# Expert stage of a mixture-of-experts decoder step: lists two steps ahead, rows fetched in mid-step, down projection by rows in split halves

## The reference

```python
gprob = softmax(x @ w_rg + b_rg); gp, gidx = top_k(gprob, 1)            # 1 of 4 groups
ep, eidx = top_k(softmax(expert logits of that group), 2)               # 2 of its 4 experts
weights = gp * ep / sum(ep)
# for each of 16 experts, c = its column of the combine weights (0 where it wasn't chosen)
y = (silu(x @ w_gate) * (x @ w_up)) @ w_down                            # 1024 -> 512 -> 1024
acc = acc + c[:, None] * y
out = rmsnorm(x_residual + acc, final_g)
```

## Time and profile before

| | us |
|---|---|
| median of 3 runs | 1002.19 |
| lowest and highest | 999.67, 1006.11 |
| the profiled execution's own time | 999.66 |
| its span, first to last instruction | 997.9 |
| first gate product of the expert stage | 499.78 |
| TensorE busy, share of the span | 910.3, 91% |
| VectorE | 465.1, 47% |
| ScalarE | 307.9, 31% |
| GpSimd | 202.3, 20% |

### The profile page before, as it was taken

One profiled execution on the slowest core, in us unless ns is written; L12 is line 12 of the kernel. 1 busy time (PEld: TensorE's weight loads), 2 busy tenths in 40 slices (PEclk: granted clock), 3 DMA queues, 4 the chain that ended last, 5 costly groups with the idle time before them and its releaser, 6 DMA issues. The chain is left out here.

```text
span 997.9 us, 15701 instructions
## 1 busy us (share of the span) xinstructions
PE 910.3 (91%) x5829; PEld 788.3 (79%) x5829; DVE 465.1 (47%) x1168; ACT 307.9 (31%) x625; POOL 202.3 (20%) x255
## 2 busy tenths in 40 slices
PE   5998999999999699997199999999999999999992
PEld 3577775666667487885199999999999999999992
DVE  4428634436864444644634434444434444433342
ACT  5546214333535422543002221222221222221121
POOL 1000000000000100000123334443334443334441
PEclk9998999999998799998599999999999999999997
DMA  8410005101010280733147698777798777798750
GB/s 269 130 43 21 22 1 126 43 1 43 1 43 1 74 310 1 279 144 106 54 162 252 239 310 280 255 241 272 266 320 275 262 255 270 254 321 298 252 175 29
DMA packets 126885, 167.05 MB, mean 167 GB/s; under 512 B 14996, under 2 KB 98040, under 8 KB 126853
## 3 DMA queue, kind: packets, MB, share of 16 engines
q1 hardware_dynamic: 111493, 136.03, 41.0%
q0 software_dynamic: 15360, 30.59, 9.0%
HBM read 147.39 MB, written 41.17 MB: 189 GB/s over the span
## 5 line engine op out<-in xcount | busy, mean ns | idle before, releaser
L1649 PE MATMUL bank<-xT,ring 128*128 128x160 f32 x2048 | 287.4, 301 | 0.7 <-issue 0.7
L1649 PEld LDWEIGHTS bank<-xT,ring 128*128 128x128 f32 x2048 | 280.8, 191 | 3.4 <-issue 3.1
L419 PE MATMUL bank<-hT,ring 128*128 128x384 f32 (+1 forms) x480 | 152.5, 472 | 0.0
L1658 PE MATMUL bank<-hid,wdn 128*128 128x160 f32 x1024 | 147.0, 299 | 0.0
L1658 PEld LDWEIGHTS bank<-hid,wdn 128*128 128x128 f32 x1024 | 140.9, 190 | 0.0
L419 PEld LDWEIGHTS bank<-hT,ring 128*128 128x128 f32 x480 | 90.6, 192 | 53.6 <-issue 4.1
L1568 POOL DMA_INDIRECT out<-ot,lists_out x64 | 87.8, 1371 | 19.8 <-issue 19.8
L1754 ACT ACTIVATE sg<-bank 128x160 f32<-128x160 f32 x64 | 19.4, 303 | 212.1 <-PE bank L1649 207.8
L1851 DVE TENSOR_TENSOR hid<-sg,bank 128x160 f32<-128x160 f32 x64 | 20.6, 321 | 111.4 <-ACT sg L1754 111.3
L1869 DVE COPY yT<-bank 128x256 f32<-128x256 f32 x32 | 13.6, 424 | 121.5 <-PE bank L1658 121.5
L1236 PE MATMUL bank<-whi,ahi 128*128 128x512 f32 (+1 forms) x144 | 57.7, 401 | 6.7 <-DVE wlo L1347 6.6
(11 more groups left out here) (316 smaller groups left out, 1311.8 us busy)
## 6 DMA issues: line engine op xcount, KB each, us to landing
wdn<-in_w_down SPq DMA_DIRECT2D x32, 1024.0 KB, 8.2
ring<-in_w_gate SPq DMA_DIRECT2D x32, 1024.0 KB, 6.3
ring<-in_w_up SPq DMA_DIRECT2D x32, 1024.0 KB, 12.3
x<-in_x_prompt SPq DMA_DIRECT2D x16, 512.0 KB, 7.0
ring<-in_w_in SPq DMA_DIRECT2D x8, 1024.0 KB, 8.8
ring<-in_w_out SPq DMA_DIRECT2D x4, 1024.0 KB, 4.9
h_rows<-h SPq DMA_DIRECT2D x8, 512.0 KB, 2.6
sums<-x SPq DMA_DIRECT2D x8, 512.0 KB, 3.6
```

The lines of the kernel that those rows point to most:

```text
L419: mm = nc.tensor.matmul(acc(n)[:, 0:tn], ring[:, u % 4, k, c0:c0 + P], hT[:, k, t0:t0 + tn], start=k == 0, stop=k == KC - 1)
L1649: x = nc.tensor.matmul(bank[f % 2][:, side * 256:side * 256 + W], ring[:, u, k, c0:c0 + P], xT[:, k, :], start=k == 0, stop=k == KC - 1)
L1658: x = nc.tensor.matmul(bank[2 + j % 2][:, q * 256:q * 256 + W], wdn[:, d // 4, k * 512 + (d % 4) * P:k * 512 + (d % 4 + 1) * P], hid[:, k, ...
```

## The change

The expert stage is moved by one step, and the down projection is turned round.

- Lists are made two steps ahead. `lists` and `weight` now belong to the expert after the next; copies `lists_next` and `lists_now` follow. VectorE computes `indices(i + 2)` at the end of step i, after waits for `old` and for the rows of `xg`, and before `z2`. The one-hot comparison stands behind the second `hid`.
- GpSimd fetches `old` straight after the scatters, once z has landed in `sums`, without waiting for the scatters of `ot`. It fetches `xg` last, for the expert two steps ahead.
- The down projection of the main rows gives rows: the stationary operand is `hid` (128 rows), the moving one `wdn`, 512 columns. Both are split into a rounded half and the rest (`wdhi`, `wdlo`, `hs`, type fp32r), and three products of the halves replace one float32 product: 2 x 4 x 3 = 24 products. ScalarE makes the rounded halves, VectorE the differences.
- The leftover rows' down projection is four strips of 32 columns of the array (`left_down`), in float32, 16 products of 256 columns.
- The transposes back, `yT` and `yT2` are gone. `left_sums` moves from the next step's first gate product to the end of its own step.
- Down weights are loaded as two halves of the hidden rows, so that one DMA run is 4 KB instead of 2 KB, both after the leftover product and the last difference.
- `old`, `z`, `ot`, `squares` and `gfb` lie in memory that held the residual rows.

```diff
@@ expert_unit
-    return wdn[:, u - 4, :].rearrange("p (k n) -> p k n", k=4), w[e, :, :, (u - 4) * 512:(u - 3) * 512]
+    return wdn[:, u - 4, :].rearrange("p (k n) -> p k n", k=2), w[e, :, 2 * (u - 4):2 * (u - 3), :]
@@ sync
-                sp.wait_ge(e_gu if u < 4 else e_yt, i * 4 + (2 if u in (0, 1, 4) else 4))
+                if u < 4:
+                    sp.wait_ge(e_gu, i * 4 + (2 if u < 2 else 4))
+                elif u == 4:
+                    sp.wait_ge(e_yl, i + 1)
+                    sp.wait_ge(e_wl, i * 4 + 4)
@@ gpsimd, the loop
             hold()
-            send(1, sums_dram, N, z, z2, e_out)
+            send(1, sums_dram, N, z, z2[:], e_sum)
             send_results(e_out)
             pool.wait_ge(e_hold, i * 3 + 4)
-            pool.wait_ge(e_idx, i + 3)
-            pool.wait_ge(e_xt, i * 3 + 6)
+            pool.wait_ge(e_next, i * 2 + 4)
+            pool.wait_ge(e_sum, i * 32 + 32)
+            hold()
+            rows_old()
+            pool.wait_ge(e_out, i * 64 + 64)
+            pool.sem_inc(e_free, 1)
+            pool.wait_ge(e_hold, i * 3 + 5)
+            pool.wait_ge(e_idx, i + 4)
+            pool.wait_ge(e_xt, i * 3 + 9)
             hold()
             rows_x()
-            pool.wait_ge(e_out, i * 96 + 96)
-            pool.sem_inc(e_free, 1)
-            pool.wait_ge(e_hold, i * 3 + 5)
-            pool.wait_ge(e_now, i * 2 + 4)
-            hold()
-            rows_old()
@@ tensor
+        def down(h, k):
+            hi, lo = hs[:, k, 0, :], hs[:, k, 1, :]
+            whi, wlo = [w[:, k, h * 512:(h + 1) * 512] for w in (wdhi, wdlo)]
+            nc.tensor.matmul(bank[2 + h][:, :], hi, whi, start=k == 0, stop=False)
+            nc.tensor.matmul(bank[2 + h][:, :], hi, wlo, start=False, stop=False)
+            x = nc.tensor.matmul(bank[2 + h][:, :], lo, whi, start=False, stop=k == 3)
+            if k == 3:
+                x.then_inc(e_y, 1)
+        def left_down():
             for k in range(4):
+                for j in range(4):
+                    at = (k % 2) * D + j * CW
+                    x = nc.tensor.matmul(bank[1][W2 * j:W2 * (j + 1), 0:CW], hid[:, k, P:W],
+                                         wdn[:, k // 2, at:at + CW], start=k == 0, stop=k == 3)
+            x.then_inc(e_yl, 1)
@@ tensor, step: after the four gate and up products
+            pe.wait_ge(e_oh, i + 3)
+            pe.wait_ge(e_idx, i + 2)
+            indices()
+            pe.wait_ge(e_xg, i * 16 + 32)
+            rows_in(i * 16 + 32)
+            pe.wait_ge(e_h, i * 4 + 5)
+            left_down()
+            for h in range(2):
+                for k in range(4):
+                    if h == 0:
+                        pe.wait_ge(e_wl, i * 4 + k + 1)
+                        pe.wait_ge(e_hl, i * 4 + k + 1)
+                    down(h, k)
+            pe.wait_ge(e_xe, i * 3 + 6)
+            pe.wait_ge(e_sql, i + 1)
+            left_sums()
@@ scalar, in the loop over f, after Silu
+                for k in ((0,), (1,), (2, 3), ())[f]:
+                    if k % 2 == 0:
+                        act.wait_ge(e_w[4 + k // 2], i * 16 + 16)
+                    nc.scalar.copy(wdhi[:, k, :], wdn[:, k // 2, (k % 2) * D:(k % 2 + 1) * D]).then_inc(e_wh, 1)
+                act.wait_ge(e_h, i * 4 + f + 2)
+                nc.scalar.copy(hs[:, f, 0, :], hid[:, f, 0:P]).then_inc(e_hh, 1)
@@ vector
+        def gated_lo(i, f):
+            dve.wait_ge(e_hh, i * 4 + f + 1)
+            nc.vector.tensor_tensor(hs[:, f, 1, :], hid[:, f, 0:P], hs[:, f, 0, :].bitcast(F32),
+                                    ALU.subtract).then_inc(e_hl, 1)
+        def weights_lo(i, k):
+            dve.wait_ge(e_wh, i * 4 + k + 1)
+            nc.vector.tensor_tensor(wdlo[:, k, :], wdn[:, k // 2, (k % 2) * D:(k % 2 + 1) * D],
+                                    wdhi[:, k, :].bitcast(F32), ALU.subtract).then_inc(e_wl, 1)
@@ vector, in the loop over f, after hid
+                gated_lo(i, f)
+                for k in ((0,), (1,), (2, 3), ())[f]:
+                    weights_lo(i, k)
+                if f == 1:
+                    dve.wait_ge(e_rk, i + 2)
                     dve.wait_ge(e_ix, i + 2)
-                    indices(i + 1)
                     onehot((i + 2) % NE)
@@ vector, after x_out
             dve.wait_ge(e_free, i + 1)
+            dve.wait_ge(e_next, i * 2 + 2)
+            nc.vector.tensor_copy(lists_now[:], lists_next[:]).then_inc(e_now, 1)
+            nc.vector.tensor_copy(weight_now[:], weight_next[:]).then_inc(e_now, 1)
+            dve.wait_ge(e_now, i * 2 + 2)
             dve.wait_ge(e_old, i * 32 + 32)
+            dve.wait_ge(e_xg, i * 16 + 32)
+            dve.wait_ge(e_xl, i * 16 + 32)
+            dve.wait_ge(e_idx, i + 2)
+            nc.vector.tensor_copy(lists_next[:], lists[:]).then_inc(e_next, 1)
+            nc.vector.tensor_copy(weight_next[:], weight[:]).then_inc(e_next, 1)
+            dve.wait_ge(e_next, i * 2 + 4)
+            dve.wait_ge(e_ix, i + 3)
+            indices(i + 2)
```

More of the change, by code:

```diff
@@ L113, in program @@
                sums_dram, rank_m, table, iota_w, steps, once)
-        b3_all(nc, A, O, sb, sem, e_w, ring, wdn, bank, ident, eps_c, h2_dram, sums_dram, rank_m, table, iota_w, steps, once)
+        b3_all(nc, A, O, sb, sem, e_w, ring, wdn, bank, ident, eps_c, x1, h2_dram, sums_dram, rank_m, table, iota_w, steps, once)
 def b1_all(nc, A, O, S0, Sp, s_w, halves, sb, sem, bank, ident, onesf, eps_c, uT, gT, ring, x1, w_in, w_out, x_rows, cols):
@@ L1465, in expert_unit, with b3_all @@
     w = A["w_down"].rearrange("l e (k p) n -> (l e) p k n", p=P)
-    return wdn[:, u - 4, :].rearrange("p (k n) -> p k n", k=4), w[e, :, :, (u - 4) * 512:(u - 3) * 512]
-def b3_all(nc, A, O, sb, sem, e_w, ring, wdn, bank, ident, eps_c, h2_dram, sums_dram, rank_m, table, iota_w, steps, once):
+    return wdn[:, u - 4, :].rearrange("p (k n) -> p k n", k=2), w[e, :, 2 * (u - 4):2 * (u - 3), :]
+def b3_all(nc, A, O, sb, sem, e_w, ring, wdn, bank, ident, eps_c, rows, h2_dram, sums_dram, rank_m, table, iota_w, steps, once):
     c3 = ExitStack()
@@ L1492, in b3_all @@
     hid = sb("hid", [P, 4, W], ctx=c3)
-    yT = sb("yT", [P, KC, P], ctx=c3)
-    yT2 = sb("yT2", [P, 2, 4, W2], ctx=c3)
-    old = sb("old", [P, D], ctx=c3)
+    hs = sb("hs", [P, 4, 2, P], F32R, ctx=c3)
+    wdhi = sb("wdhi", [P, 4, D], F32R, ctx=c3)
+    wdlo = sb("wdlo", [P, 4, D], F32R, ctx=c3)
+    old, z, ot, squares, gfb = [rows[:, j, :] for j in range(5)]
     old2 = sb("old2", [P, CW], ctx=c3)
-    z = sb("z", [P, D], ctx=c3)
     z2 = sb("z2", [P, CW], ctx=c3)
-    ot = sb("ot", [P, D], ctx=c3)
     ot2 = sb("ot2", [P, CW], ctx=c3)
-    squares = sb("squares", [P, D + CW], ctx=c3)
+    squares2 = sb("squares2", [P, CW], ctx=c3)
     ssq = sb("ssq3", [P, 4], ctx=c3)
@@ L1562, in rows_old @@
         def rows_old():
-            fetch(old[:], sums_dram, lists_now, 0, e_old)
-            fetch(old2[:], parts(sums_dram), lists_now, 1, e_old)
+            fetch(old, sums_dram, lists_next, 0, e_old)
+            fetch(old2[:], parts(sums_dram), lists_next, 1, e_old)
         def send(kind, dst, rows, main, left, signal):
@@ L1595, in _ @@
         rows_x()
+        pool.wait_ge(e_hold, 1)
+        pool.wait_ge(e_next, 2)
+        hold()
         rows_old()
+        pool.wait_ge(e_hold, 2)
+        pool.wait_ge(e_idx, 3)
+        pool.wait_ge(e_xt, 6)
+        hold()
+        rows_x()
         with pool.Fori(0, n - 1) as i:
             pool.wait_ge(e_hold, i * 3 + 3)
-            pool.wait_ge(e_last, i + 1)
+            pool.wait_ge(e_now, i * 2 + 2)
             pool.wait_ge(e_z, i * 3 + 4)
@@ L1703, in step @@
                     pe.wait_ge(e_w[f + 1], i * 16 + 16)
+                if f == 1:
+                    pe.wait_ge(e_z, i * 3 + 1)
                 gate_up(f, 0)
[L1705 to L1708 removed]
                 if first and f == 0:
@@ L1712, in step @@
                     indices()
[L1713 to L1725 removed]
+                gate_up(f, 1)
             pe.wait_ge(e_oh, i + 3)
@@ L1742, in _ @@
             step(i, False)
-        pe.wait_ge(e_sq, n * 3 + 1)
-        left_sums()
     @blk.scalar
@@ L1847, in _ @@
         lower(1)
+        dve.wait_ge(e_xg, 16)
+        dve.wait_ge(e_xl, 16)
+        dve.wait_ge(e_idx, 1)
+        nc.vector.tensor_copy(lists_next[:], lists[:]).then_inc(e_next, 1)
+        nc.vector.tensor_copy(weight_next[:], weight[:]).then_inc(e_next, 1)
+        dve.wait_ge(e_next, 2)
+        dve.wait_ge(e_ix, 2)
+        indices(1)
         with dve.Fori(0, n) as i:
@@ L1886, in _ @@
             dve.wait_ge(e_z, i * 3 + 4)
-            for c, (out, src, g) in enumerate(((ot, z, gfb), (ot2, z2, gf2))):
+            for c, (out, src, g) in enumerate(((ot, z, gfb), (ot2[:], z2[:], gf2[:]))):
                 dve.wait_ge(e_rt, i * 2 + c + 1)
```

141 lines of the change are left out of this document (36 added, 105 removed).

## The result

The change makes the kernel faster: 963.11 us, median of 4 runs (961.96 to 969.26), against 1002.51 for the kernel before beside it (999.67 to 1006.11), a ratio of 0.962 with a 95% interval of 0.955 to 0.968. The forecast was 1031; the rival "faster" had 953, range 945 to 968. The profiled execution is the longest of the four, 969.26 us, span 967.5; two more executions on record, outside the median, took 957.12 and 970.42.

What follows compares the result with a forecast made beforehand. TensorE and the loop over `sums`, `old` and z were held level; after the change the loop, 7.85 + 15.7 + 6.4 + 2.4 = 32.35 us against TensorE's 26.7, sets steps, giving 1031 us, range 990 to 1056.

Steps and rivals of the forecast that it cites:

- the rival "faster": New differences block little or not, `old` goes out ahead of the gate loads, TensorE sets the step: 953 us, chance 0.20.
- I take 4.0: GpSimd's transfers between hold and the second fetch of `old`: four VectorE differences block them for 4.0 us, bounds 0 and 5.9.
- So the blocking costs twice: Blocking also puts the second `old` fetch at 21 us, behind the gate loads, instead of 17.2; flight taken as 6.4.
- z2 to hold: VectorE's path from z2 through both halves of z to hold: 3.05 us plus 4.8, together 7.85.
- After a first free step the loop sets the rest: Steps of the expert stage: first 26.7 us, then 14 of 32.3 set by the `sums` loop, 478.9 against 448.75.
- The clock: TensorE idling 5.6 us per step may fall to 1.2 GHz: some 1.8 us a fall, at most +1.7 per step.
- The last `hid` and SP's queue: VectorE's last `hid` at about 19.0 us and SP's waiting down loads were both taken to cost TensorE nothing.
- ScalarE's wait for the down weights: ScalarE's first copy waits for the down weights; costed at nothing, their late landing named as what would break the forecast.
- TensorE's 26.7: TensorE's list of work per step after the change: 26.7 us, against 29.6 before.
- the strips at 2.05: Leftover rows' down product on TensorE: four strips run together and cost 2.05 us, or 7.0 if they did not.
- Rival (3): `old` behind the gate loads flies only 3.9 to 4.7 us: loop 29.9 to 30.7, 1001 to 1013 us, chance 0.14.
- Rival (4): TensorE's strips do not run together: its list takes 31.7 us, 1029 in all, chance 0.04.

## Why the prediction was wrong

**The step that failed** is "I take 4.0", the blocking of GpSimd's transfers by the four differences. That they block was right, and the bounds (0 to 5.9) held; the measured value is 0 in the path of `old` in short steps (11.45 us from hold to the second fetch against 11.7 without blocking) and 2.3 in long ones (716.22 - 702.26 = 13.96). Two things were overlooked. The price was worked out for each operation as if transfers fell on it at random, but the transfers stand at fixed places in the step, started by a chain that hangs on the last down product (z of the second half follows it at 756.76), next to which stand `left_sums` and the gates that lead to the differences; in the short step shown they miss by 0.05 to 0.08 us. And delays were added up, where one that falls ahead of the comparison, an obstacle that stops the queue until a fixed time, is absorbed by it: with the comparison held 2.25 us in any case, what the first two differences cost ahead of it is free up to that time.

**What hung on it.** "So the blocking costs twice" was right in the main: it matters whether the second fetch is ahead of the second pair of gate loads. At 17.1 us against 17.9 it is, with 0.8 us to spare (the text had 1.5, for blocking and flight together). Behind the loads `old` flies 7.0 to 7.3 us in the three long steps, against 6.4 taken. Ahead of them it flies 3.8 to 5.3 in ten of twelve steps, but 6.3 in one and 7.2 in the one from 641.65, where `left_sums` waits 0.73 us; so being ahead doesn't make it safe, and why those two are slow is open. z2 to hold is 7.4 us where the loop runs late (725.67 to 733.10), not 7.85.

**"After a first free step the loop sets the rest"** took for granted that what is once late stays late. It holds where each step has 5 us more on GpSimd's path, or where z2 is uncoupled from the lists; in the changed kernel it doesn't: the lateness is gone after two or three steps.

**The clock** was costed at 1.8 us for a fall, which none of the rows shown gives, and 1.7 a step at most. The fall shown above cost 2.5 us of gate products (20.10 against 17.63).

**What was costed at nothing.** The last `hid` and SP's queue were nothing in the changed kernel. ScalarE's wait for the down weights, listed at the end as what would break the forecast, was not: three waits of some 0.6 us cost 17.6 us of the profiled execution, 12 of the median. The rival "faster" had 953 without them; with the down weights in time the median is 951.22. The two loads are issued at 777.84 in the short step, 3 us behind two gate loads of the same size; over all steps they land in 7.7 to 13.0 us.

**What was right.** TensorE's 26.7 (26.73 measured; the list of the kernel before was given as 29.6, though its terms add up to 29.3, which changes nothing here), the strips at 2.05 (1.93), the differences at 1.22, ScalarE's room. So was the rule of the Trainium skill's page "SBUF — State Buffer", section "SBUF: two separate sides", that two SBUF operands make the block: 1.24 to 3.38 us with them, 0.98 with one operand in PSUM. It says what blocks and until when; what a block costs the step hangs on what the held transfer would have waited for next. Rival (3) rested on the Trainium skill's page "DMA: Bandwidth & Descriptors", section "Queues, rings and completion order", with its rotation packet by packet. The rival's 3.9 to 4.7 us behind the gate loads isn't borne out, it was 7.0 to 7.3; whether the DMA engines rotate no run shows. Rival (4) was excluded by the 1.93.

The chance of 0.20 for the rival "faster" was too low for a term with bounds of 0 and 5.9 and a switch at 1.5: where the sum changes sign inside the bounds of one unknown, that unknown has to be laid out along the step, transfer by transfer, before a value is taken.

## What to carry to other kernels

Where two engines exclude each other, don't multiply the number of operations by a mean delay: draw both queues for one step, move each held transfer, and see which later wait swallows it. A loop between steps that has 0.8 us of room is fast, but a load that is 0.55 us late can cost six over two steps, and one that is 1.42 late, in a variant of the same kernel, nothing; look in the groups for small waits that occur only a few times, and match them with the long steps. And before a faster version of an operation is built, restore the old length of the engine's list in an experiment: it tells at once whether anything else was gained.

## What was unexpected of the hardware

- Four independent accumulations in strips of 32 columns take 1.93 us when issued in turn and 4.59 when each strip's eight records follow each other: here strips overlap fully only when neighbouring records go to different strips. The 4.59 is still less than the 7.0 estimated for none together, and why is open.
- The wait of 3.24 us on TensorE was followed by some 5 us at 1.2 GHz, and the next step was 3.09 us longer than a short one, so that the wait cost about twice its length.
- A `left_sums` that is released at the last moment costs 0.6 us even where the timeline shows no wait: the gates behind it begin after 0.76 to 0.81 us instead of 0.14. The cause is open.
- In the kernels with later down loads, strips in sequence and the doubled product, the third Silu starts 14.5 us into the step instead of 13.46 (the profile has it waiting for the gate product), though ScalarE's program and the gates are the same, and TensorE then waits 0.42 us for the last `hid`. The kernel with one product less has the same delay of about a microsecond between its second and third Silu. The cause is open; it makes some 6 us of the times of the first three.
